# Attention queries kept in both partition halves and split by one operation, and gate tiles dealt by TensorE's work alone

## The chip, the cores and the metric

One core of one Trainium2 chip runs the whole kernel. Time is the device time of one execution in microseconds; a profile of one execution gives the rows below. The engines run side by side and meet at semaphores: TensorE (PE, its weight loads PEld), VectorE (DVE), ScalarE (ACT), GpSimd (POOL) and SyncE (SP), which issues most DMAs.

## The reference, cut to what matters

A decoder layer over 512 tokens of width 2048: a normed input goes through one wide projection; its parts feed sparse attention (16 heads of 64 in 4 groups; compressed, selected and window keys), a spatial-gating MLP and two merge gates; then come cross-attention, a SwiGLU and a last norm. The change touches the attention and the projection of the merge gates that runs beside it.

```python
h = rmsnorm(x, norm_mix_g[l])
proj = h @ w_in[l]
q, kv, nsa_g, u, v, merge_g = jnp.split(proj, split_points, axis=-1)
...
# per query block of 128, per group and head:
s_c = jnp.einsum('bghqd,bgnd->bghqn', qb, kc)
p_c = masked_softmax(s_c, cmp_end[None, :] <= t[:, None])
o_c = jnp.einsum('bghqn,bgnd->bghqd', p_c.astype(vc.dtype), vc)
...
# the same for the selected keys (all blocks here, causal) and the window keys
out = gates[..., 0:1] * unblock(o_c) + gates[..., 1:2] * unblock(o_s) + gates[..., 2:3] * unblock(o_w)
...
g = jax.nn.sigmoid(merge_g).reshape(b, s, N_BRANCHES, D_MODEL)
merged = g[:, :, 0] * (o_a @ w_proj_a[l]) + g[:, :, 1] * (o_b @ w_proj_b[l])
```

## The kernel before

Every float32 operand of a matrix product is split into a high part and a low remainder, and a product is three matmuls: high with high, high with low, low with high. The work is written out by hand, engine by engine; the order on each engine is the order of the code, and semaphores tie the engines together.

Projection phases run one after another: `m0` and the Strassen-like products `g` (which also make the queries and store them to `q_dram`), then `c` (keys and values to be compressed), `k`, `v`, `g` (branch gates), and then the attention stage. A weight panel of 2048 rows by 128 columns is loaded into one of two `raw` slots by SyncE, split in four quarters by VectorE (`split`: a cast at L1504 and a subtraction at L1506) and used by TensorE (L986 to L988). A quarter of the split weights is free again when TensorE has used it.

The attention stage has 128 steps. A unit is two heads of one query block of 128 tokens (`HALVES`, 32 units, 8 for each query block `qi` of 0 to 3); its scores are made in 2, 4, 4 or 5 steps, growing with the causal length (`SCORES`). In each step TensorE does, in this order: a third of the step's gate tiles, the scores of this step (L1194, `scores`), a third of the gate tiles, a turn (`turn_probs`, L1207 and L1210: transposes of scaled probabilities of the unit before), the last third, and `weigh` (L1221 and L1225): the product with the values for what was turned in the step before. Between a turn and its `weigh` ScalarE copies the high part out of the bank (L2474) and VectorE makes the low part (L1763), so `weigh` waits for VectorE.

A gate tile is one k-row of 128 of the merge gates' projection: three matmuls of 512 columns that wait for nothing of the attention. There are 256 of them, 64 quarters, dealt over the 128 steps by `spread` (`TILES_AT`); after each whole quarter VectorE splits the quarter three ahead, at the end of its own work in that step (`QUARTERS_AT`), and after each whole panel ScalarE copies the result (L2311) and stores it. `spread` deals by the mean of two fits: one that evens TensorE's work per step (`step_cost`), one that follows VectorE's work per step (`step_vector`), so that steps in which VectorE has much to do get many tiles and others one or none.

VectorE's order in a step is: row maxima of the scores (L1735), the unit's coefficients (L1747, L1751), the queries' low part for the next unit (`query_low`, L1710), the low part of the turn (L1763), the sum of an output (L1770), splits. ScalarE's is: the queries' high part (`query_high`, L2421, first in a step of `qi` 0, behind the exponentials otherwise), the copy of the turn, the exponentials (L2456), an output copy (L2482), a gate copy. GpSimd scales the probabilities by the coefficients (L2820, L2825).

The keys lie in a tile of 128 partitions, high part in one half and low in the other, so a query has to stand in both halves. Before, `q_t` holds all queries once: partition half `e` is the head `e` of a pair, and one DMA (L785) fills it. For each unit four operations on ScalarE and four on VectorE, each of 64 partitions by 128 columns, take a head from its half and put it into one half of `q_hl`.

Of the kernel before, what the change touches and what calls it, by code (L numbers as in the profile page):

```python
# [162 lines left out]
def step_vector(step):  # L163

    cost = 0
    hu, part = STEP_OF[step] if step < len(STEP_OF) else (len(HALVES), step - len(STEP_OF))
    if step < len(STEP_OF):
        cost += sum(700 + 2 * (NCP if b == CMP else (HALVES[hu][2] + 1) * P) for _, b in SCORES[hu][part])
    if part == 0 and 0 < hu <= len(HALVES):
        cost += 600  # L170
    if hu + 1 < len(HALVES) and part == (0 if len(SCORES[hu]) == 2 else 2):
        cost += 4 * 700
    if step in TURN_AT:
        own, k = TURN_AT[step]
        cost += 460 + 4 * P * max(1, len(turns(HALVES[own][2])[k]))
    if step - 1 in CLOSE_AT:
        cost += 2 * 640
    return cost


def spread(tiles, costs, others):

    each, own = 3 * T, 660

    def even(ratio, other):
        return [max(0.0, (ratio * o - c) / max(each - ratio * w, 1)) for c, o, w in other]

    def fitted(other):
        low, high = 0.0, 2.0 * max(costs) + 4.0 * each
        for _ in range(80):  # L190
            ratio = (low + high) / 2
            low, high = (ratio, high) if sum(even(ratio, other)) < tiles else (low, ratio)
        return even(ratio, other)
    by_pe = fitted([(c, 1, 0) for c in costs])
    by_vector = fitted([(c, o, own) for c, o in zip(costs, others)])
    wanted = [(a + b) / 2 for a, b in zip(by_pe, by_vector)]
    at, left, goal = [], list(range(tiles)), 0.0
    for step, want in enumerate(wanted):
        goal += want
        n = len(left) if step == len(costs) - 1 else min(len(left), max(0, round(goal) - (tiles - len(left))))  # L200
        at.append(left[:n])
        left = left[n:]
    return at
# [33 lines left out]
def build(nc, x, mem, norm_mix_g, w_in, cmp_pe_k, cmp_k_w1, cmp_k_b1, cmp_k_w2, cmp_pe_v, cmp_v_w1,  # L237
# [5 lines left out]
    with ExitStack() as ctx:  # L243
# [53 lines left out]
        q_t = at("q_t", [P, 8, T], F32, C)  # L297
# [328 lines left out]

        def kv_panel(p):
            return (PH["mk"] if p < 4 else PH["mv"],) + PH["mk"].at(p % 4)

        G_UNITS = 7 * G_PAIRS  # L630
        J11, J22, J22S, J12, JZ, J21 = range(1, 7)
        def g_join(what, p):
# [2315 lines left out]
```

## Time and profile before

| what | value |
|---|---|
| median of 3 runs | 2784.32 us (2784.04 to 2785.43) |
| profiled execution, its own time | 2784.62 us |
| its span, first to last instruction | 2782.9 us, 1.7 us less |
| TensorE matmul busy | 2727.8 us, 98% |
| VectorE busy | 2136.2 us, 77% |
| ScalarE busy | 1180.0 us, 42% |
| chain that ended last | TensorE 84%, VectorE 7%, ScalarE 3%, DMA 2%, GpSimd 2% |

The attention stage stands between 481 and 819 us of the span. Busy times of matmuls overlap a little (they are pipelined), so a stall of TensorE is read best from the idle time before its weight loads.

### The profile page before, as it was taken

The page shows a single profiled execution, that of the slowest core. Times are in us where ns is not written, and L with a number is a line of the kernel's source. Part 1 is how long each engine was busy: PE and PEld are TensorE (multiplying, and loading weights), DVE is VectorE, ACT ScalarE, POOL GpSimd, SP SyncE. Part 2 cuts the span into 40 slices and gives each one's busy share as a digit, 9 for nine tenths or more (in the row PEclk, how much of TensorE's full clock was granted, in tenths as well). Part 3 has the DMA queues.
Part 4 walks back from the last instruction along what each step waited for, and adds up shares of the span by engine and source line. Part 5 has one row for each costly group of instructions (what it writes and reads, how often), then busy time and mean ns, then how long its engine had stood idle before and what let it go on. Part 6 is the DMA issues. An engine that isn't in the chain of part 4 may idle for free.

```text
span 2782.9 us, 38124 instructions
## 1 busy us (share of the span) xinstructions
PE 2727.8 (98%) x14157; PEld 2306.9 (83%) x14157; DVE 2136.2 (77%) x3158; ACT 1180.0 (42%) x1935; POOL 449.9 (16%) x414
## 2 busy tenths in 40 slices
PE   8999999999999999999999999999999999999998
PEld 7888887778778888888877888888888888788886
DVE  6777653878764555565678899999999999988887
ACT  6444311656640322211144455555555555443334
POOL 0000020445540454511000000000000000010000
PEclk9999999999999999999999999999999999999999
DMA  7588652222223444544334788888888888899882
GB/s 240 141 188 176 174 144 53 75 73 62 54 68 104 107 130 141 145 120 116 94 118 133 176 204 221 200 217 200 209 217 203 214 202 261 299 293 303 291 267 92
DMA packets 629641, 467.83 MB, mean 168 GB/s; under 512 B 14068, under 2 KB 572008, under 8 KB 623592
## 3 DMA queue, kind: packets, MB, share of 16 engines
q1 hardware_dynamic: 561232, 412.39, 50.2%
q0 software_dynamic: 54736, 34.61, 9.5%
q10 hardware_dynamic: 13512, 18.68, 1.9%
q8 instruction: 102, 1.67, 0.2%
q14 instruction: 59, 0.48, 0.1%
HBM read 404.55 MB, written 61.08 MB: 167 GB/s over the span
## 4 chain that ended last, share of the span: by engine, by line
PE 84%; DVE 7%; ACT 3%; issue 2%; DMA 2%; POOL 2%; ACTq 0%; DVEq 0%; SPq 0%; POOLq 0%
PE banks L986 10%; PE banks L988 10%; PE banks L987 10%; PE banks L1425 9%; PE banks L1422 9%; PE banks L1423 9%; PE banks L1487 4%; PE banks L1488 4%; PE banks L1489 4%; PE banks L1084 2%; PE banks L1087 2%; PE banks L1085 2%; PE banks L1253 1%; PE banks L1254 1%; PE banks L1255 1%
## 5 line engine op out<-in xcount | busy, mean ns | idle before, releaser
L1504 DVE CAST w_hi<-raw 128x512 fp32r<-128x512 f32 (+1 forms) x328 | 186.3, 568 | 304.6 <-PE banks L988 233.1
L986 PE MATMUL banks<-act_hl,w_hi 128*128 128x512 f32 (+1 forms) x944 | 374.5, 397 | 2.4 <-DVE w_lo L1525 2.4
L988 PE MATMUL banks<-act_hl,w_lo 128*128 128x512 f32 (+1 forms) x944 | 368.8, 391 | 0.0
L987 PE MATMUL banks<-act_hl,w_hi 128*128 128x512 f32 (+1 forms) x944 | 368.7, 391 | 0.0
L1423 PEld LDWEIGHTS banks<-t_hl,wf_lo 128*128 128x128 f32 x1312 | 246.5, 188 | 58.3
L1425 PE MATMUL banks<-t_hl,wf_hi 128*128 128x512 f32 x656 | 259.4, 396 | 0.0
L1422 PE MATMUL banks<-t_hl,wf_hi 128*128 128x512 f32 x656 | 259.3, 395 | 0.0
L1506 DVE TENSOR_TENSOR w_lo<-raw,w_hi 128x512 fp32r<-128x512 f32 (+1 forms) x328 | 249.6, 761 | 11.3
L1423 PE MATMUL banks<-t_hl,wf_lo 128*128 128x256 f32 x1312 | 257.7, 278 | 0.0
L1972 DVE TENSOR_TENSOR wf_lo<-raw_f,wf_hi 128x1024 fp32r<-128x1024 f32 x164 | 200.3, 1222 | 56.7 <-ACT wf_hi L2621 56.6
L2621 ACT ACTIVATE wf_hi<-raw_f 128x1024 fp32r<-128x1024 f32 x164 | 173.8, 1060 | 136.9 <-PE banks L1425 83.7
L1423 PEld LDWEIGHTS banks<-tok_hl,wf_lo 128*128 128x128 f32 x984 | 184.8, 188 | 43.7
L1487 PE MATMUL banks<-wo_hi,h_full 128*128 128x512 f32 x560 | 219.0, 391 | 1.4 <-DVE wo_lo L2006 1.4
L1489 PE MATMUL banks<-wo_lo,h_full 128*128 128x512 f32 x560 | 218.0, 389 | 0.0
L1488 PE MATMUL banks<-wo_hi,h_full 128*128 128x512 f32 x560 | 217.9, 389 | 0.0
L988 PEld LDWEIGHTS banks<-act_hl,w_lo 128*128 128x128 f32 (+1 forms) x944 | 176.1, 187 | 39.4
L986 PEld LDWEIGHTS banks<-act_hl,w_hi 128*128 128x128 f32 (+1 forms) x944 | 176.4, 187 | 33.0 <-issue 2.6
L987 PEld LDWEIGHTS banks<-act_hl,w_hi 128*128 128x128 f32 (+1 forms) x944 | 176.6, 187 | 30.3
L1425 PE MATMUL banks<-tok_hl,wf_hi 128*128 128x512 f32 x492 | 194.6, 396 | 0.0
L1422 PE MATMUL banks<-tok_hl,wf_hi 128*128 128x512 f32 x492 | 194.4, 395 | 0.0
L1423 PE MATMUL banks<-tok_hl,wf_lo 128*128 128x256 f32 x984 | 193.3, 278 | 0.0
L2621 ACT ACTIVATE wf_hi<-s 128x1024 fp32r<-128x1024 f32 x123 | 130.2, 1058 | 137.9 <-PE banks L1425 137.9
(361 smaller groups left out, 6142.8 us busy)
## 6 DMA issues: line engine op xcount, KB each, us to landing
raw_f<-in_w_ffn_in_dram SPq DMA_DIRECT2D x82, 1024.0 KB, 9.0
raw<-in_w_in_dram SPq DMA_DIRECT2D x50, 1024.0 KB, 5.6
h_full<-hidden_blocks SPq DMA_DIRECT2D x35, 1024.0 KB, 7.8
wo_raw<-in_w_ffn_out_dram SPq DMA_DIRECT2D x32, 1024.0 KB, 10.0
hidden_blocks<-tok_hl SPq DMA_DIRECT2D x44, 512.0 KB, 6.2
s<-in_w_ffn_in_dram SPq DMA_DIRECT2D x40, 512.0 KB, 5.9
s<-in_w_ffn_in_dram POOLq DMA_DIRECT2D x40, 512.0 KB, 6.5
raw_g<-in_w_in_dram SPq DMA_DIRECT2D x18, 1024.0 KB, 8.8
```

Source lines behind the costliest of these rows:

```text
L986: pe.matmul(dst, w_hi[:, q, j, 0:m], hi, start=first, stop=False)
L987: pe.matmul(dst, w_hi[:, q, j, 0:m], lo, start=False, stop=False)
L988: return pe.matmul(dst, w_lo[:, q, j, 0:m], hi, start=False, stop=last)
L1422: pe.matmul(dst, w_h[:, k], both(k), start=start and k == 0, stop=False, skip_group_check=True)
L1423: mm = pe.matmul(dst[:, 0], w_l[:, k], both(k)[:, 0], start=False, stop=False, skip_group_check=True)
L1425: mm = pe.matmul(dst, w_h[:, k], both(k), start=False, stop=last, skip_group_check=True)
L1487: pe.matmul(dst, hi, wo_hi[g % 3][:, k], start=STARTS[j] and q == 0 and k == 0, stop=False, skip_group_check=True)
L1488: pe.matmul(dst, lo, wo_hi[g % 3][:, k], start=False, stop=False, skip_group_check=True)
L1489: mm = pe.matmul(dst, hi, wo_lo[g % 3][:, k], start=False, stop=last, skip_group_check=True)
L1506: dve.tensor_tensor(w_lo[:, q, :, 0:width], src, w_hi[:, q, :, 0:width].bitcast(F32), ALU.subtract).then_inc(split_done, 1)
L1972: dve.tensor_tensor(wf_lo[g % 3][:].rearrange("p k n -> p (k n)"), src, wf_hi[g % 3][:].rearrange("p k n -> p (k n)").bitcast(F32), ALU.su ...
L2621: act.activation(wf_hi[g % 3][:].rearrange("p k n -> p (k n)"), src, ACT.Copy).then_inc(f_hi, 1)
```

## The change

The queries of a query block are loaded twice, once into each partition half: `q_t` becomes 2 slots (query blocks, in turn) of 16 heads by 128 tokens, the same 16 KiB per partition. Four DMAs on SyncE's queue, each of 64 partitions, fill both slots where one DMA stood; blocks 2 and 3 are loaded by two DMAs each from ScalarE's queue, behind the first high part of blocks 1 and 2. With both heads in both halves, one operation of 128 partitions by 2x128 makes the high part of a unit on ScalarE and one the low part on VectorE. `spread` loses its second fit: tiles are dealt so that TensorE's work by `step_cost` is even over the steps. The number of tiles and of splits is the same.

```diff
@@ step_vector and spread
-def step_vector(step):
-
-    cost = 0
...
-    if hu + 1 < len(HALVES) and part == (0 if len(SCORES[hu]) == 2 else 2):
-        cost += 4 * 700
...
-def spread(tiles, costs, others):
-
-    each, own = 3 * T, 660
...
-    by_pe = fitted([(c, 1, 0) for c in costs])
-    by_vector = fitted([(c, o, own) for c, o in zip(costs, others)])
-    wanted = [(a + b) / 2 for a, b in zip(by_pe, by_vector)]
...
+def spread(tiles, costs):
+
+    each = 3 * T + 96
+    total = sum(costs) + tiles * each
+    at, left, spent = [], list(range(tiles)), 0
+    for step, cost in enumerate(costs):
+        spent += cost
+        goal = total * (step + 1) / len(costs)
+        n = 0 if step < len(costs) - 1 else len(left)
+        while n < len(left) and spent + n * each < goal:
+            n += 1
+        spent += n * each
         at.append(left[:n])
         left = left[n:]
     return at
@@ build: the queries' tile and the dealing
-        q_t = at("q_t", [P, 8, T], F32, C)
+        q_t = at("q_t", [P, 2, HEADS, P], F32, C)
...
-        TILES_AT = spread(GATE_TILES, [step_cost(step) for step in range(STEPS)], [step_vector(step) for step in range(STEPS)])
+        TILES_AT = spread(GATE_TILES, [step_cost(step) for step in range(STEPS)])
...
+        def query(hu):
+            j, pr, qi = HALVES[hu]
+            head = 2 * (2 * j + pr)
+            return q_t[:, qi % 2, head:head + 2]
...
+        q_v = q_dram.rearrange("(a p) t -> p a t", p=HD)
@@ SyncE
-            sp.dma_start(q_t[:], q_dram.rearrange("(k p) t -> p k t", p=P)).then_inc(q_landed, 16)
+            for qi in range(2):
+                for h in range(2):
+                    sp.dma_start(q_t[h * HD:(h + 1) * HD, qi], q_v[:, :, qi * P:(qi + 1) * P]).then_inc(q_landed, 16)
@@ TensorE, scores
-                    pe.wait_ge(q_lo, 4 * hu + 4)
+                    pe.wait_ge(q_lo, hu + 1)
@@ VectorE, query_low
-                for e in range(2):
-                    rows = slice(e * HD, (e + 1) * HD)
-                    for h in range(2):
-                        dve.wait_ge(q_hi, 4 * hu + 2 * e + 2)
-                        dve.scalar_tensor_tensor(out=q_hl[h * HD:(h + 1) * HD, hu % 2, e, 1], in0=q_t[rows, 2 * j + pr, qi * P:(qi + 1) * P],
-                                                 scalar=-HD ** -0.5, in1=q_hl[rows, hu % 2, e, 0].bitcast(F32),
-                                                 op0=ALU.mult, op1=ALU.subtract).then_inc(q_lo, 1)
+                dve.wait_ge(q_hi, hu + 1)
+                dve.scalar_tensor_tensor(out=q_hl[:, hu % 2, :, 1], in0=query(hu), scalar=-HD ** -0.5, in1=q_hl[:, hu % 2, :, 0].bitcast(F32),
+                                         op0=ALU.mult, op1=ALU.subtract).then_inc(q_lo, 1)
@@ ScalarE, query_high
-                if hu == 0:
-                    act.wait_ge(q_landed, G_DMA0 + 16)
+                act.wait_ge(q_landed, G_DMA0 + 32 * max(qi + 1, 2))
                 wait(act, qk_done, STEP0[max(hu - 1, 0)])
-                for e in range(2):
-                    for h in range(2):
-                        act.activation(q_hl[h * HD:(h + 1) * HD, hu % 2, e, 0], q_t[e * HD:(e + 1) * HD, 2 * j + pr, qi * P:(qi + 1) * P], ACT.Copy, scale=-HD ** -0.5).then_inc(q_hi, 1)
+                act.activation(q_hl[:, hu % 2, :, 0], query(hu), ACT.Copy, scale=-HD ** -0.5).then_inc(q_hi, 1)
+                if j == pr == 0 and qi in (1, 2):
+                    act.wait_ge(q_lo, hu)
+                    for h in range(2):
+                        act.dma_start(q_t[h * HD:(h + 1) * HD, (qi + 1) % 2], q_v[:, :, (qi + 1) * P:(qi + 2) * P]).then_inc(q_landed, 16)
```

TensorE, in the steps 93 to 95 of 128 (query block 3). `q_hl` marks the scores, `ident` the turn, `prob_t` the weighing, and three rows with `act_hl` are one gate tile. Before:

```order
3041 L1194 MATMUL banks<-k_win,q_hl 128x512 x2
3042 L1210 MATMUL banks<-ident,prob 128x128 x4
3043 L1225 MATMUL banks<-prob_t,v_hl 128x256 x4
3044 L1194 MATMUL banks<-k_win,q_hl 128x512 x2
3045 L1210 MATMUL banks<-ident,prob 128x128 x4
3046 L1225 MATMUL banks<-prob_t,v_hl 128x256 x4
3047 L986 MATMUL banks<-act_hl,w_hi 128x512
3048 L987 MATMUL banks<-act_hl,w_hi 128x512
3049 L988 MATMUL banks<-act_hl,w_lo 128x512
```

After, the same steps:

```order
2990 L1175 MATMUL banks<-k_win,q_hl 128x512 x2
2991 L967 MATMUL banks<-act_hl,w_hi 128x512
2992 L968 MATMUL banks<-act_hl,w_hi 128x512
2993 L969 MATMUL banks<-act_hl,w_lo 128x512
2994 L1191 MATMUL banks<-ident,prob 128x128 x4
2995 L1206 MATMUL banks<-prob_t,v_hl 128x256 x4
2996 L967 MATMUL banks<-act_hl,w_hi 128x512
2997 L968 MATMUL banks<-act_hl,w_hi 128x512
2998 L969 MATMUL banks<-act_hl,w_lo 128x512
2999 L1175 MATMUL banks<-k_win,q_hl 128x512 x2
3000 L1191 MATMUL banks<-ident,prob 128x128 x4
3001 L1206 MATMUL banks<-prob_t,v_hl 128x256 x4
```

Step 94 had no tile and has one now, and step 93 has one more between its scores and its turn; between the turn of step 93 and the weighing of what it turned, which is the next but one, there is a tile where there was none.

VectorE, in step 92 of the same stage (the step with the queries of the next unit). Before:

```order
988 L1735 ISA banks,attn_max<-banks,causal 128x512
989 L1735 ISA attn_max 128x1
990 L1710 SCALAR_TENSOR_TENSOR q_hl<-q_t,q_hl 64x128 x4
991 L1763 TENSOR_TENSOR prob_t<-banks,prob_t 128x512
992 L1770 TENSOR_TENSOR oa<-banks,o_low 64x128 x2
993 L1504 CAST w_hi<-raw 128x512
994 L1506 TENSOR_TENSOR w_lo<-raw,w_hi 128x512
```

After:

```order
980 L1710 ISA banks,attn_max<-banks,causal 128x512
981 L1710 ISA attn_max 128x1
982 L1686 SCALAR_TENSOR_TENSOR q_hl<-q_t,q_hl 128x2x128
983 L1738 TENSOR_TENSOR prob_t<-banks,prob_t 128x512
984 L1745 TENSOR_TENSOR oa<-banks,o_low 64x128 x2
985 L1485 CAST w_hi<-raw 128x512
986 L1487 TENSOR_TENSOR w_lo<-raw,w_hi 128x512
```

The four query operations have become one in the same place; the rest of this step is as it was.

SyncE, behind the last panel of phase `c`. Before:

```order
56 L783 DMA w_101<-in_cmp_k_w_dram 128x2x64
57 L783 DMA w_101<-in_cmp_v_w_dram 128x2x64
58 L785 DMA q_t<-queries 128x8x512
59 L606 UNCONDITIONAL_BRANCH
60 L606 ISA
```

After:

```order
56 L762 DMA w_101<-in_cmp_k_w_dram 128x2x64
57 L762 DMA w_101<-in_cmp_v_w_dram 128x2x64
58 L766 DMA q_t<-queries 64x16x128 x4
59 L580 UNCONDITIONAL_BRANCH
60 L580 ISA
```

The same 2 MB (two of four query blocks, twice) now come in pieces of 512 bytes instead of 2 KB, ahead of the first panel of phase `k`.

## Rows read from the trace of the kernel before

**Rows 1.** The page, busy time by engine.

```profile
PE 2727.8 (98%) x14157; PEld 2306.9 (83%) x14157; DVE 2136.2 (77%) x3158; ACT 1180.0 (42%) x1935; POOL 449.9 (16%) x414
```

**Rows 2.** Busy times in the attention stage: PE, PEld, DVE, ACT, POOL, clock, DMA.

```profile
480.00:820.00 340.00, 321.70 (x1827) 267.27 (x1825) 268.17 (x878) 208.33 (x672) 167.08 (x193) 1.00 0.22 62
```

**Rows 3.** Waits of the weight loads in the attention stage: us, times, longest.

```profile
PEld banks L1225 <- DVE prob_t L1763: 26.1, 39, 1.4
PEld banks L1207 <- POOL prob_c L2820: 2.6, 6, 0.9
PEld banks L1210 <- POOL prob L2825: 2.1, 4, 0.8
```

**Rows 4.** Timeline of weight loads, steps 93 to 95: start, us, instruction [idle before].

```profile
736.93 0.58 PEld L1210 LDWEIGHTS banks<-ident,prob 128*128 128x128 f32 x4
...
738.30 0.59 PEld L1210 LDWEIGHTS banks<-ident,prob 128*128 128x128 f32 x4
740.25 0.53 PEld L1225 LDWEIGHTS banks<-prob_t,v_hl 128*128 128x128 f32 x4 [1.36 <-DVE prob_t L1763]
...
742.80 0.54 PEld L1225 LDWEIGHTS banks<-prob_t,v_hl 128*128 128x128 f32 x4 [0.49 <-DVE prob_t L1763]
```

**Rows 5.** Timeline of VectorE, end of step 92 and step 93.

```profile
737.21 0.59 DVE L1770 TENSOR_TENSOR oa<-banks,o_low 64x128 f32<-64x128 f32 x2
737.83 0.43 DVE L1504 CAST w_hi<-raw 128x512 fp32r<-128x512 f32 x1
738.29 0.69 DVE L1506 TENSOR_TENSOR w_lo<-raw,w_hi 128x512 fp32r<-128x512 f32 x1
738.90 0.69 DVE L1735 CUSTOM_DVE_ANT_0 banks<-banks,causal 128x512 f32<-128x512 f32 x1
...
739.51 0.69 DVE L1763 TENSOR_TENSOR prob_t<-banks,prob_t 128x512 fp32r<-128x512 f32 x1
```

**Rows 6.** Groups by shape in the stage, 480 to 815 us.

```profile
L1763 DVE TENSOR_TENSOR prob_t<-banks,prob_t 128x512 fp32r<-128x512 f32 x79 | 54.4, 689 | 20.3 <-ACT prob_t L2474 18.8
L2474 ACT ACTIVATE prob_t<-banks 128x512 fp32r<-128x512 f32 x79 | 47.1, 597 | 39.0 <-PE banks L1210 34.1 <-ACT gate_out L2311 2.4 <-PE banks L1225 1.9
L1710 DVE SCALAR_TENSOR_TENSOR q_hl<-q_t,q_hl 64x128 fp32r<-64x128 f32 x124 | 40.8, 329 | 6.9 <-ACT q_hl L2421 3.9
L2421 ACT ACTIVATE q_hl<-q_t 64x128 fp32r<-64x128 f32 x124 | 37.9, 306 | 2.7 <-ACT gate_out L2311 0.4
```

**Rows 7.** The queries' low parts: ns min/median/max, then a quick and a slow unit.

```profile
L1710 DVE SCALAR_TENSOR_TENSOR q_hl<-q_t,q_hl x128: 275/288/815, 457.9 to 786.5; 64x128 fp32r<-64x128 f32 x128
...
482.71 1.24 DVE L1710 SCALAR_TENSOR_TENSOR q_hl<-q_t,q_hl 64x128 fp32r<-64x128 f32 x4
...
773.14 1.76 DVE L1710 SCALAR_TENSOR_TENSOR q_hl<-q_t,q_hl 64x128 fp32r<-64x128 f32 x4
```

**Rows 8.** SyncE's issues at L785 and L746 (first panel of k), each with its landing.

```profile
344.55 0.71 SPq L785 DMA_DIRECT2D q_t<-queries  x1
DMA to landing us min/median/max: 11.7/11.7/11.7
...
346.02 2.25 SPq L746 DMA_DIRECT2D raw<-in_w_in_dram  x1
DMA to landing us min/median/max: 13.8/13.8/13.8
```

**Rows 9.** Windows while queries, then the panel land; the last two columns are DMA share and GB/s.

```profile
350.00:355.00 5.00, 5.00 (x23) 4.13 (x22) 2.01 (x4) 2.37 (x4) 0.00 (x0) 1.00 1.05 386
355.00:360.00 5.00, 5.00 (x24) 4.13 (x22) 0.15 (x1) 0.00 (x0) 0.00 (x0) 1.00 1.19 296
```

**Rows 10.** Timeline of VectorE and ScalarE where phase k begins.

```profile
359.85 0.43 DVE L1504 CAST w_hi<-raw 128x512 fp32r<-128x512 f32 x1 [6.21 <-DMA raw<-in_w_in_dram]
360.31 0.69 DVE L1506 TENSOR_TENSOR w_lo<-raw,w_hi 128x512 fp32r<-128x512 f32 x1
...
363.46 0.59 ACT L2388 ACTIVATE kv_src<-banks 64x512 f32 x1 [8.47 <-PE banks L988]
```

## What the change does to the time, predicted before it ran

> **What bounds the kernel now.** I read the page first, then the waits, and the rows of single steps last. The page shows TensorE busy for 98% of the span [rows 1], so only what TensorE works, or waits for, can move the time. The change takes no matmul away: the same 256 gate tiles, scores, turns and weighings stand in the new order. What it can win is TensorE's idle time in the attention stage, what it can lose is new idle time there or in the phases before.
>
> The window over the stage has TensorE at full clock, 2.4 GHz (granted 1.00), VectorE busy 268.2 of 340 us, ScalarE 208.3, GpSimd 167.1 [rows 2]. No helper is full, yet TensorE waits. Its matmul rows would show 18.3 us idle (340 - 321.7), but a matmul's recorded end hides part of a stall, so I take the waits of the weight loads: 26.1 us in 39 waits of `weigh` for VectorE's low part, and 2.6 + 2.1 us in 10 waits of the turns for GpSimd's scaling, 30.8 us together [rows 3]. That is 1.1% of the span and the most that the stage can give back. Without it a step takes (340 - 30.8) / 128 = 2.4 us on TensorE.
>
> Steps 93 to 95 show how such a wait comes about. After the turn at 738.30 the weights of `weigh` are loaded at 740.25, 1.36 us late, and one step on again 0.49 us late [rows 4]. VectorE meanwhile makes an output sum, a quarter's split (737.83 to 738.98) and the row maxima, and reaches the awaited low part only at 739.51, ending at 740.20 [rows 5]. Step 94 has no gate tile, so TensorE got to its `weigh` with nothing to pass the time. Placing all waits of the stage in the order of steps gives the rule that I rest on: of the 39 waits for VectorE all but one begin in, or right behind, a step with at most one tile. Counted in TensorE's order, 65 of the 128 steps are such steps before (3, 11, 15 and 31 in query blocks 0 to 3, 5 in the steps behind), because the dealing gave the step with the queries and the sums 3 to 5 tiles and its neighbours one or none. So a step with at most one tile costs 26.1 / 65 = 0.40 us.
>
> **The even dealing.** After, 24 steps have one tile, none has none (2, 2, 6, 14 and 0), and 80 have two. From turn to `weigh` the helpers need 0.60 us for the copy and 0.69 us for the low part [rows 6], 1.3 us, plus what VectorE has queued. TensorE meanwhile passes the weighing before, the scores, the next turn and the tiles. Without a tile that is 1.4 us, from the end of the turn's loads at 737.5 to the arrival at 740.25 - 1.36 = 738.9 [rows 4]. A tile adds 0.65 us (23 to 24 matmuls of 512 columns pass in 5 us [rows 9], and a tile is three), so one tile gives 2.05 and two give 2.7 us. Two tiles leave 1.4 us, which covers a split (0.46 + 0.69 us) [rows 5]; one leaves 0.75 us, which does not. I therefore keep the price of 0.40 us for the 24 steps: 9.6 us. Bounds: nothing, if the lighter queries below free VectorE in time; and 26.1 us, if the waits move to the steps with two tiles.
>
> The waits for GpSimd (4.7 us) also fall in steps that TensorE reaches early, after one-tile steps. By the count they would shrink to 24/65, 1.7 us; but units of block 3, where they are longest, now pass in the same time as before or less, and GpSimd's own work is unchanged. I take 3 us, between 1.7 and 4.7.
>
> **The queries' operations.** Per unit four VectorE operations of 64x128 become one of 128x2x128. Four take 1.24 us in a quick unit and 1.76 in a slow one [rows 7]. No row shows the new shape. It has two inputs in SBUF as the old one has. From below it costs as the old one, 0.29 us; from above, twice it with the worst old duration, 1.6 us, hence no gain. The nearest rows are the old 0.29 us for 128 columns and the low part of a turn, 0.69 us for 512: one operation of 256 columns lies between, near 0.42 us. VectorE then has some 0.8 to 1.3 us less per unit, 31 units in the stage, 25 to 40 us; take 29: 239 of 322 us, 74% instead of 79%. On ScalarE four copies of 0.31 us [rows 6] become one of about 0.4 us, 0.8 us less per unit. Neither engine is the bound, so this adds no term of its own: its value is a shorter queue ahead of the low part in one step of each unit, and it cancels what the 80 steps with two tiles might cost (one of 18 such steps waited before, 1.26 us; at that rate 80 would cost 5.6 us).
>
> An operation's length varies: 275 ns at least, 288 in the median, 815 at most [rows 7], the long ones while GpSimd scales probabilities. One operation instead of four can be held up once instead of four times; the worst seen adds 0.53 us, which a step with two tiles bears.
>
> **The queries' load.** This is the part that can cost. SyncE issues the old load at 344.55, it lands after 11.7 us at 356.25, and behind it the first weight panel of phase `k` lands at 359.82 [rows 8]. VectorE waits 6.2 us for that panel and has its first quarter at 361.0; TensorE has finished phase `c` at 363.4, where ScalarE is released [rows 10]. So the panel has 2.4 us of slack, and TensorE stalls by what the panel is later than that. Panel and queries share the DMA engines, which are full: 386 GB/s while the queries move in 2 KB pieces, 296 GB/s while the panel moves in 512-byte pieces [rows 9]. The new load has the same 2.1 MB in 512-byte pieces: at 296 GB/s it takes 7.1 us instead of 5.4, and the panel comes 1.7 us later: no stall. From above, at half that rate (each DMA fills 64 partitions only, and no row shows such a load) 14.2 us, 8.8 us later, a stall of 6.4 us. From below nothing, since an earlier panel helps no one. I take the row of the same piece size, 0, and keep 6.4 as the end. The three more issues (0.37 to 0.71 us each when the queue is free) lie behind transfers that are still running.
>
> A rule of the Trainium skill speaks against that choice: "SBUF — State Buffer", section on the DMA port swizzle, says that partitions 0 to 63 reach only 8 of the 16 ports, measured there as 196 against 328 GB/s for 1 MiB. By it the load would take some 10.7 us, an estimate, the panel would be 5.3 us late, and TensorE would stall 2.9 us. No load of 64 partitions is in this trace, so the row of 296 GB/s neither supports nor refutes it; as a mechanism of this kernel it is rival 2 below.
>
> The four later DMAs on ScalarE's queue are issued one unit ahead; the two issues of a block cost ScalarE some 0.7 us twice, at 61% busy in the stage [rows 2], and their data have a whole query block less one unit to land. The wait for `q_lo` ahead of them is met by VectorE's operation of an earlier step. Both: nothing.
>
> **The sum.** 30.8 us of waits now; 9.6 + 3 us left, so 18.2 us less; load 0. Against the profiled execution's own 2784.62 us that makes 2766.4; the median of the runs is 0.3 us lower, and the forecast is 2766 us.
>
> **The rivals.** A measurement of this kernel tells a change from none at about 0.2%, 5.6 us, so from 2778.7 to 2789.9 is the same.
> 1. Half the gain: the waits for VectorE move to steps with two tiles that also carry a split. For: every second step now carries a split and no step gets extra tiles for it. Against: 1.4 us of room against 1.15 us of split. 0.2 us in each of 80 steps, less the part that the forecast already has, gives 9 us back: 2775.
> 2. The load of 64 partitions at a time runs slower than any row here. Midway between the ends of 0 and 6.4 us TensorE stalls 3 us ahead of `k`, the rest as forecast: 2769, at most 2773. For: every DMA of the stage's rows fills all partitions, and none shows that half of them will do as well. Against: only that the piece size alone explains the row of 296 GB/s.
> 3. No change: the wait is the length of copy and low part, wherever the tiles stand, and moves with them: 2784. Against: steps with 3 to 5 tiles had no wait.
> 4. Slower: VectorE becomes late for good. Its step with the queries has maxima, query, low part, two sums and a split, some 3.2 us, against 2.4 us of TensorE, and no longer 3 or 4 tiles to cover it. If it does not catch up before the next split, each of the 64 quarter splits holds a `weigh` by some 0.6 us: 38 us against 30.8 removed, 2792. It decides from a mean of 30.8 / 64 = 0.48 us per split. Against: VectorE's 74% mean load, and steps without a split that take it 1.3 us.
>
> **How the numbers follow.** Forecast 0.58, rival 1 0.16, rival 2 0.07, rival 3 0.11, rival 4 0.08. Faster: 0.58 + 0.15 + 0.07 = 0.80; the same: 0.11 and a hundredth of rival 1, 0.12; slower 0.08. The forecast's own range is 2758 (all but 4 us of the waits gone) to 2775. For 8 in 10 it takes in rivals 1 and 2 and the edge of 3: 2756 to 2780.
>
> **What would show it.** Right: weight loads in the stage wait under 15 us, most of it in steps with one tile; the stage is about 18 us shorter; the query operations are 31 of 0.4 to 0.5 us on VectorE; the first panel of `k` lands within 2.4 us of its old time and no TensorE wait stands there. Wrong: waits of `weigh` in steps with two tiles, more than 0.1 us each on average; or GpSimd named as the releaser for more than 5 us; or a wait of TensorE for a split at the start of `k`. VectorE's rows at about 0.7 us per query operation would mean that the shape was mis-sized, but not the time.

## The result, and the profile after

The changed kernel takes 2769.37 us in the median of 5 runs (2768.63 to 2771.49), the kernel before 2784.32: a ratio of 0.9946 with an interval of 0.9931 to 0.996, some 15 us less. The forecast was 2766. The profiled execution took 2769.78 us with a span of 2768.1, 14.8 us less than the one before.

The page's engine row of the kernel after answers to [rows 1]: busy time, share of the span, instructions.

```profile
PE 2723.1 (98%) x14157; PEld 2306.4 (83%) x14157; DVE 2113.2 (76%) x3062; ACT 1150.0 (42%) x1839; POOL 455.6 (16%) x414
```

TensorE has the same 14157 matmuls and is still the bound. VectorE has 96 instructions fewer (3158 to 3062), which are the three query operations saved in each of 32 units, and works 23.0 us less; ScalarE has the same 96 fewer.

The window over the attention stage after, columns as in [rows 2]:

```profile
484.00:806.00 322.00, 316.45 (x1832) 266.62 (x1831) 245.84 (x786) 180.11 (x580) 170.94 (x193) 1.00 0.27 72
```

The waits of the weight loads in it, as in [rows 3]: us, times, longest.

```profile
PEld banks L1191 <- POOL prob L2801: 6.0, 12, 1.6
PEld banks L1206 <- DVE prob_t L1738: 5.3, 10, 1.0
PEld banks L1188 <- POOL prob_c L2796: 2.4, 8, 0.4
```

From the first scores to the first weight load behind the stage it was 339.1 us (481.3 to 820.4) and is 320.2 (485.1 to 805.2): 18.9 less. These are the first starts in the rows of the scores and of the phase behind the stage (ns min/median/max, first and last start), before:

```profile
L1194 PEld LDWEIGHTS banks<-k_sel,q_hl x160: 186/188/192, 481.3 to 796.2; 128*128 128x128 f32 x160
L1253 PEld LDWEIGHTS banks<-w_hi,act_hl x128: 187/188/190, 820.4 to 907.6; 128*128 128x128 f32 x128
```

and after:

```profile
L1175 PEld LDWEIGHTS banks<-k_sel,q_hl x160: 186/188/192, 485.1 to 777.6; 128*128 128x128 f32 x160
L1234 PEld LDWEIGHTS banks<-w_hi,act_hl x128: 186/188/190, 805.2 to 892.4; 128*128 128x128 f32 x128
```

The three kinds of waits went from 30.8 to 13.7 us, which is 17.1 of it. But the stage also begins 3.8 us later, so 15.1 us remain for the whole. Two things differ from the forecast in these rows: GpSimd holds more than VectorE does (8.4 against 5.3 us; before it was 4.7 against 26.1), and something ahead of the stage has lost almost 4 us.

That loss stands where phase `k` begins. Windows of the kernel after, while queries and panel land [rows 9] and behind it:

```profile
350.00:355.00 5.00, 5.00 (x23) 4.13 (x23) 2.02 (x4) 2.37 (x4) 0.00 (x0) 1.00 1.21 207
355.00:360.00 5.00, 5.00 (x23) 4.13 (x22) 0.00 (x0) 0.00 (x1) 0.00 (x0) 1.00 1.21 209
...
366.00:368.00 2.00, 2.00 (x7) 1.58 (x8) 1.97 (x3) 0.00 (x0) 2.00 (x3) 0.67 0.54 132
368.00:370.00 2.00, 2.00 (x6) 1.61 (x5) 1.97 (x3) 0.00 (x0) 2.00 (x3) 0.50 0.00 0
370.00:372.00 2.00, 2.00 (x10) 1.55 (x10) 1.97 (x3) 0.00 (x0) 2.00 (x3) 0.97 0.00 0
```

The timeline there, for ScalarE's first copy behind phase `c`, VectorE, TensorE's weight loads and its first matmul [rows 10]:

```profile
363.47 0.59 ACT L2363 ACTIVATE kv_src<-banks 64x512 f32 x1 [8.47 <-PE banks L969]
...
364.63 0.43 DVE L1485 CAST w_hi<-raw 128x512 fp32r<-128x512 f32 x1 [10.97 <-DMA raw<-in_w_in_dram]
365.09 0.69 DVE L1487 TENSOR_TENSOR w_lo<-raw,w_hi 128x512 fp32r<-128x512 f32 x1
...
365.90 0.19 PEld L967 LDWEIGHTS banks<-act_hl,w_hi 128*128 128x128 f32 x1 [2.98 <-ACT kv_src L2364]
...
365.93 0.47 PE L967 MATMUL banks<-act_hl,w_hi 128*128 128x512 f32 x1 [2.58 <-ACT kv_src L2364]
```

The queries move at 207 to 209 GB/s, where they moved at 386 before and where the row of the same piece size had 296. Phase `c` ends at the same time as before (363.47 against 363.46), but the first panel's cast begins at 364.63 instead of 359.85, 4.8 us later. That is more than the 2.4 us of slack, so TensorE idles 2.6 us. The row names ScalarE as the releaser, but the instruction before the restart is VectorE's low part, which ends at 365.78: a wait for several semaphores is put down to one of them, and the one that decided must be read from the times. Behind the idle stretch the granted clock falls to 0.67 and then 0.50, which is 1.2 instead of 2.4 GHz, and is back at 0.97 from 370 on; at those levels 23 matmuls pass in the 6 us shown where some 28 would at the full clock (23 to 24 in 5 us [rows 9]), an estimate of about 1 us, which is the rest of the 3.8.

SyncE's issues, as in [rows 8], show the same from the queue's side. The line for the four query loads: ns min/median/max, first and last start.

```profile
L766 SPq DMA_DIRECT2D q_t<-queries x4: 732/2070/2960, 344.5 to 350.0; - x4
```

The first issue takes 0.73 us, as the one before did (0.71); those behind it, made while the loads ahead of them are under way, take up to 3.0 us. The panel behind them is issued only at 353.2 (before at 346.0).

The query operations themselves, as in [rows 7]: ns min/median/max.

```profile
L1686 DVE SCALAR_TENSOR_TENSOR q_hl<-q_t,q_hl x32: 415/421/894, 462.4 to 765.9; 128x256 fp32r<-128x256 f32 x32
```

On ScalarE the 32 high parts have a median of 403 ns (before 308 for each of 128). Both sizes were forecast (0.42 and about 0.4 us).

### The profile page after: what moved, and what is told of

Read it like the earlier page. It is cut to its first block, busy times and chain, and to the rows that moved or that the text cites. A ratio compares the mean times of both kernels' runs of the same rounds, so it can differ in the third digit from the quotient of the medians.

```text
span 2768.1 us, 37969 instructions
## 1 busy us (share of the span) xinstructions
PE 2723.1 (98%) x14157; PEld 2306.4 (83%) x14157; DVE 2113.2 (76%) x3062; ACT 1150.0 (42%) x1839; POOL 455.6 (16%) x414
## 4 chain that ended last, share of the span: by engine, by line
PE 86%; DVE 5%; ACT 2%; issue 2%; POOL 2%; DMA 2%; ACTq 0%; DVEq 0%; SPq 0%; POOLq 0%
PE banks L967 10%; PE banks L968 10%; PE banks L969 10%; PE banks L1406 9%; PE banks L1403 9%; PE banks L1404 9%; PE banks L1468 4%; PE banks L1469 4%; PE banks L1470 4%; PE banks L1065 2%; PE banks L1068 2%; PE banks L1066 2%; PE banks L1175 1%; PE banks L1206 1%; PE banks L1234 1%
```

## The experiments

Every timed run stands beside runs of the kernel before on the same chip (2785.6 to 2785.8 us); ratios go by those.

**The two halves of the change by themselves.** `queries_alone` is the kernel after with the old dealing; `dealing_alone` is the kernel before with the new one.

```diff
@@ queries_alone, against the kernel after
-        TILES_AT = spread(GATE_TILES, [step_cost(step) for step in range(STEPS)])
+        TILES_AT = spread(GATE_TILES, [step_cost(step) for step in range(STEPS)], [step_vector(step) for step in range(STEPS)])
@@ dealing_alone, against the kernel before: the same line the other way; each with the spread that belongs to it
```

> The changed kernel with the old dealing of gate tiles (the fit that follows VectorE's work is back), so the queries' part alone. Theory A, that the waits of weigh come from steps with at most one gate tile: the 65 such steps are back, the lighter query operations shorten only part of the queue, 20 to 26 us of waits stay in the attention stage, and the load costs its 3.8 us ahead of phase k: 2778 to 2784 us. Theory B, that the four query operations on VectorE and ScalarE were what made TensorE wait: waits near 14 us as in the changed kernel, 2769 to 2773 us.

> The kernel before with the new dealing alone (four query operations per engine and unit, one query load of 2 KB pieces). Theory A (tiles): most of the 30.8 us of waits go, 12 to 18 us stay, no stall ahead of phase k: 2766 to 2772 us. Theory B (query operations): 25 us or more stay, 2779 to 2784 us.

Measured: `queries_alone` 2778.55 us, ratio 0.9974 (0.9964 to 0.9985); `dealing_alone` 2777.28 us, ratio 0.9969 (0.9957 to 0.9982). Waits of the weight loads in the stage, first `queries_alone`:

```profile
PEld banks L1232 <- DVE prob_t L1764: 16.1, 28, 1.4
PEld banks L1214 <- POOL prob_c L2822: 2.8, 6, 0.9
PEld banks L1217 <- POOL prob L2827: 2.1, 4, 0.8
```

and `dealing_alone`:

```profile
PEld banks L1199 <- DVE prob_t L1737: 15.3, 20, 1.8
PEld banks L1184 <- POOL prob L2799: 5.4, 11, 1.5
...
PEld banks L1181 <- POOL prob_c L2794: 1.1, 4, 0.4
PEld banks L1195 <- DVE pc_t L1735: 0.6, 1, 0.6
```

In one table (us; waits are those for VectorE and GpSimd; a wait of 1.1 us for ScalarE's gate copy stands at the end of the stage and is left out):

| kernel | waits for VectorE | for GpSimd | together | stage |
|---|---|---|---|---|
| before | 26.1 | 4.7 | 30.8 | 339.1 |
| queries alone | 16.1 | 4.9 | 21.0 | 329.0 |
| dealing alone | 15.9 | 6.5 | 22.4 | 331.2 |
| both (after) | 5.3 | 8.4 | 13.7 | 320.2 |

Each half takes about 10 and 8 us off the stage, and the two nearly add up (10.1 + 7.9 = 18.0 against 18.9). The forecast had put the whole gain on the dealing. `queries_alone` came out in the range of its theory A, at its low end in waits (21.0 us); `dealing_alone`, at 22.4 us of waits and 2777.28 us, between its two theories.

Placing the waits in the order of steps shows where the dealing fell short. Behind step 19 it does what was forecast: the waits for the low part fall from 21.8 us to 6.6, where the price of 0.40 us for the 22 one-tile steps there would leave 8.8. In steps 7 to 19, in which TensorE weighs units of query block 0, they grow, from 4.1 us to 8.7, although the steps that wait have two or three tiles: 0.73 us in step 7, 0.32 in step 9, then 1.58, 1.58, 1.71, 0.95 and 1.82 in steps 11, 13, 15, 17 and 19. The lighter queries take most of these away: in the kernel after, steps 7 to 19 hold 3.0 us and the rest of the stage 2.3. `queries_alone` bears the dearer load of the queries as well: its TensorE idles 2.3 us ahead of `k`, so its whole-kernel gain (7 us) is smaller than that of its stage (10.1).

**The order of the loads.** `panel_ahead` is the kernel after with the first panel of `k` issued ahead of the four query loads.

```diff
+            keys_panel(0)
             for qi in range(2):
                 for h in range(2):
                     sp.dma_start(q_t[h * HD:(h + 1) * HD, qi], q_v[:, :, qi * P:(qi + 1) * P]).then_inc(q_landed, 16)
-            columns(PH["k"], w_in_v, C_KV + 2 * 256, step=2 * 256)
+            for n in range(1, PH["k"].n):
+                keys_panel(n)
```

> The changed kernel, with the first weight panel of phase k issued ahead of the four query loads on SyncE's queue. Theory P (the load of 64 partitions at 207 GB/s pushes the panel behind TensorE's need): the panel lands near 353 us, no wait of TensorE and no fall of its clock at the start of k, scores begin at 481.3 instead of 485.1 us, 3.8 us less: 2765.6 us. Rival Q (the queries delay some other panel as well, the second of k): the stall moves 11 us on and the time stays near 2769 us.

Measured: 2765.67 us (2765.58 to 2766.82), ratio 0.9927 (0.9913 to 0.994). The panel lands at 355.1 us (expected near 353), TensorE has no wait at the start of `k`, the stage begins at 480.8 instead of 485.1, and its waits are as in the kernel after (13.4 us, stage 319.9). The load costs what stood ahead of `k` and nothing else. A second run of the same kernel and one of the unchanged one came beside later experiments:

> The changed kernel with the first panel of phase k ahead of the query loads once more, as the base of the two kernels with four operations on the same chip: 13.4 us of waits in the stage, ratio to the kernel before 0.9927 to 0.993, about 2765.5 us.

> The changed kernel once more, on the same chip as the three kernels that have its first panel of phase k issued ahead of the query loads, to have its difference to them without a change of chip. By the two profiles (start of the scores 485.1 against 480.8 us, stage 320.2 against 319.9) the changed kernel is 4 us behind a kernel with the panel ahead: ratio to the kernel before 0.9945, about 2769 to 2770.

`panel_again` took 2766.16 us, ratio 0.9931 (0.9918 to 0.9945); `changed_again` 2768.49 us, a little under what was expected, ratio 0.994 (0.9926 to 0.9953). So the order of the loads is worth 2.3 to 3.7 us between medians, which come from different chips; the intervals of the ratios overlap, and it is the trace that settles it. When phase `c` ends differs from one profiled execution to the next, by up to 3.4 us (ScalarE's first copy behind it starts between 362.77 and 366.17 us), so I measure from there to the first scores: 117.1 to 117.2 us in all nine profiled executions of changed kernels without a wait at that place, `panel_ahead` and `panel_again` among them, 117.8 in the kernel before (its 0.7 us stand elsewhere and are open), 121.6 in the kernel after and 119.3 in `changed_again`. In the latter TensorE's weight loads wait 2.2 us and the clock stays up. Its window there:

```profile
365.00:370.00 5.00, 3.76 (x17) 3.14 (x18) 4.90 (x7) 1.89 (x4) 2.99 (x4) 1.00 0.59 143
```

The loss to the clock is thus not part of every execution, and the late panel costs 2.1 us in one and 4.5 us in the other.

**What makes the load slow: half the partitions, or small pieces?** `half_loads` is the kernel before with its one load cut into two of 64 partitions each, pieces of 2 KB as before. `full_width_load` is the kernel after with its four loads spread over all 128 partitions, pieces of 512 bytes as after.

```diff
@@ half_loads
-            sp.dma_start(q_t[:], q_dram.rearrange("(k p) t -> p k t", p=P)).then_inc(q_landed, 16)
+            for h in range(2):
+                sp.dma_start(q_t[h * HD:(h + 1) * HD], q_dram.rearrange("(k p) t -> p k t", p=P)[h * HD:(h + 1) * HD]).then_inc(q_landed, 16)
@@ full_width_load
-                    sp.dma_start(q_t[h * HD:(h + 1) * HD, qi], q_v[:, :, qi * P:(qi + 1) * P]).then_inc(q_landed, 16)
+                    sp.dma_start(q_t[:, qi, h * 8:(h + 1) * 8], q_w[:, :, qi * P:(qi + 1) * P]).then_inc(q_landed, 16)
```

> The kernel before, whose one query load of 128 partitions becomes two DMAs of 64 partitions each, still in 2 KB pieces. Theory P (a DMA into 64 partitions runs at about 207 GB/s whatever its pieces): the queries take some 10 us instead of 5.4, the first panel of k lands 4 to 5 us later, TensorE waits 2 to 3 us and loses about 1 us to a lower clock behind it: 2787 to 2788.5 us. Rival R (the 512-byte pieces were the cause): the load moves at 380 GB/s, the panel keeps its time, 2784.3 us.

> The changed kernel (panel behind the queries) with four DMAs of 512 KB in 512-byte pieces as before, but each into all 128 partitions, so that the queries in the tile are not those that the attention needs. Theory P (half the partitions cost the rate): the four move at 290 GB/s or more, the first panel of k lands by 362 us, no wait of TensorE at the start of k, scores begin near 481 us. Rival R (many small pieces, or four DMAs, cost it): 207 GB/s as with 64 partitions, the panel at 364 us, a wait of 2 to 3 us.

Measured: `half_loads` 2788.69 us, ratio 1.001 (1.0001 to 1.0019). `full_width_load` 2766.9 us in its one run. Windows of `half_loads`:

```profile
350.00:355.00 5.00, 5.00 (x23) 4.13 (x22) 2.24 (x4) 1.71 (x3) 0.00 (x0) 1.00 1.09 220
355.00:360.00 5.00, 5.00 (x23) 4.13 (x22) 0.00 (x0) 0.66 (x2) 0.00 (x0) 1.00 1.07 216
```

and of `full_width_load`:

```profile
350.00:355.00 5.00, 5.00 (x23) 4.13 (x22) 2.00 (x4) 0.00 (x0) 0.00 (x0) 1.00 1.17 303
355.00:360.00 5.00, 5.00 (x24) 4.14 (x23) 1.12 (x2) 2.37 (x4) 0.00 (x0) 1.00 1.20 292
```

Two-kilobyte pieces into 64 partitions move at 216 to 220 GB/s, 512-byte pieces into all partitions at 292 to 303, 512-byte pieces into 64 partitions at 207 to 209. In `queries_alone`, with the same four loads as the kernel after, these same windows show 218 and 217 GB/s, so between piece sizes no difference is seen at 64 partitions. The width of the load decides; the piece size alone would have given the 296 of [rows 9]. That there are four transfers is not the cause either, as `full_width_load` has four. `half_loads` idles TensorE 2.4 us ahead of `k` with nothing else changed, at full clock, where its theory had a fall of the clock as well; its first scores stand 120.1 us behind the end of phase `c`, 2.3 more than before, and it ends 3.1 us slower than the kernel before beside it. `full_width_load` has no wait there, as expected, but two of its expected times were missed: the first panel's cast begins at 364.04 (landing by 362) and the scores at 483.3 (near 481). This execution was 2.8 us late already when it issued the queries (347.3 against 344.5 us), and its first scores stand 117.1 us behind the end of `c`, like those of the kernels without a wait. Of the Trainium skill, "SBUF — State Buffer" says in its section on the DMA port swizzle that the rate of a DMA depends on how many ports its partitions reach, and that 64 partitions reach half of them; its section "Can I just issue two DMAs to hit both halves?" answers that two transfers, one into each half, serialize. Both agree with `half_loads`, whose two loads go to opposite halves and still move at 216 to 220 GB/s together.

**Which engine's query operations held TensorE.** Both kernels are `panel_ahead` with four operations of 64x128 again on one engine only: VectorE in `vector_four`, ScalarE in `scalar_four`.

```diff
@@ vector_four (scalar_four has the same loops around act.activation)
-                dve.scalar_tensor_tensor(out=q_hl[:, hu % 2, :, 1], in0=query(hu), ...
+                for e in range(2):
+                    for h in range(2):
+                        rows = slice(h * HD, (h + 1) * HD)
+                        a = dve.scalar_tensor_tensor(out=q_hl[rows, hu % 2, e, 1], in0=query(hu)[rows, e], ...
```

> Panel ahead, even dealing, queries in both halves; VectorE makes the low part of a unit with four operations of 64x128 again, ScalarE keeps its one. Theory VQ (the queries' part won by VectorE's shorter queue): nearly all of the 8.7 us that the lighter queries were worth under the even dealing (22.4 against 13.7 us of waits) come back: 20 to 22 us of waits, 2772 to 2774 us. Rival SQ (it won by ScalarE's, which also copies the turns): 14 to 16 us, 2766 to 2768 us.

> Panel ahead, even dealing, queries in both halves; ScalarE makes the high part with four operations of 64x128 again, VectorE keeps its one. Theory VQ: 14 to 16 us of waits, 2766 to 2768 us. Rival SQ: 20 us or more, 2772 us or more. If both four-operation kernels lose, each by its share, the chain high part, low part, scores counts, not one engine's queue.

Measured: `vector_four` 2773.6 us, ratio 0.9959 (0.9945 to 0.9972), waits 19.9 us; `scalar_four` 2772.14 us, ratio 0.9951 (0.9937 to 0.9964), waits 19.0. Against `panel_again` beside them (0.9931, 13.4 us) each costs 5.6 to 6.5 us in waits, and 6 to 7.4 us in the median. Of the growth of the waits for VectorE (7.4 and 6.8 us), 4.1 and 4.6 us stand in steps 0 to 15. Theory VQ, that only VectorE's queue counts, fails with `scalar_four`, and its rival SQ with `vector_four`: four operations hurt on either engine alone, and neither of them is full. The same step, 11 of the stage, shows why. VectorE in `panel_ahead`:

```profile
508.18 0.42 DVE L1692 SCALAR_TENSOR_TENSOR q_hl<-q_t,q_hl 128x256 fp32r<-128x256 f32 x1 [0.32 <-ACT q_hl L2399]
508.80 0.69 DVE L1744 TENSOR_TENSOR prob_t<-banks,prob_t 128x512 fp32r<-128x512 f32 x1 [0.20 <-ACT prob_t L2456]
```

VectorE in `vector_four`, and TensorE's weighing behind it:

```profile
511.24 1.30 DVE L1695 SCALAR_TENSOR_TENSOR q_hl<-q_t,q_hl 64x128 fp32r<-64x128 f32 x4 [0.32 <-ACT q_hl L2403]
512.57 0.69 DVE L1748 TENSOR_TENSOR prob_t<-banks,prob_t 128x512 fp32r<-128x512 f32 x1
...
513.32 0.53 PEld L1212 LDWEIGHTS banks<-prob_t,v_hl 128*128 128x128 f32 x4 [1.34 <-DVE prob_t L1748]
```

ScalarE, VectorE and the weighing in `scalar_four`:

```profile
510.29 1.26 ACT L2402 ACTIVATE q_hl<-q_t 64x128 fp32r<-64x128 f32 x4
511.58 0.60 ACT L2460 ACTIVATE prob_t<-banks 128x512 fp32r<-128x512 f32 x1
...
511.58 0.42 DVE L1692 SCALAR_TENSOR_TENSOR q_hl<-q_t,q_hl 128x256 fp32r<-128x256 f32 x1 [1.18 <-ACT q_hl L2402]
512.21 0.69 DVE L1744 TENSOR_TENSOR prob_t<-banks,prob_t 128x512 fp32r<-128x512 f32 x1 [0.20 <-ACT prob_t L2460]
...
512.95 0.53 PEld L1212 LDWEIGHTS banks<-prob_t,v_hl 128*128 128x128 f32 x4 [1.41 <-DVE prob_t L1744]
```

In query block 0 the high part, the low part, the turn's copy and the turn's low part are one chain over both engines. Four operations on VectorE stand ahead of the low part of the turn; four on ScalarE stand ahead of its copy and make VectorE wait 1.18 us for the queries. From the start of the query operation to the one behind it, it is 0.62 us with one operation and 1.33 with four on VectorE, and 0.43 against 1.29 on ScalarE: 0.7 and 0.9 us more. The query operation itself also starts some 0.5 us later against TensorE's scores than in `panel_ahead`. So `weigh`, which has no wait at this step in `panel_ahead`, waits 1.3 to 1.4 us. VectorE's waits for the queries' high part in the stage grow from 1.7 us (5 times) to 12.6 (17 times) in `scalar_four`:

```profile
DVE q_hl L1692 <- ACT q_hl L2402: 12.6, 17, 1.4
```

**What is a tile worth in a step?** Both are `panel_ahead` with another dealing. `refit` has the old fit with the queries' true cost in it, and 54 steps with at most one tile; `two_each` gives every step two tiles.

```diff
@@ refit, in the old step_vector
-        cost += 4 * 700
+        cost += 900
@@ two_each
+    each = tiles // len(costs)
+    return [list(range(step * each, (step + 1) * each)) for step in range(len(costs))]
```

> Panel ahead of the queries, with the old dealing (mean of TensorE's and VectorE's fit) whose cost of the queries is lowered to that of one operation, 900 in place of 2800. It has 54 steps with at most one tile (the old dealing 65, the new 24). Theory A: 54 steps cost what such steps cost beside light queries, 21.0 / 65 = 0.32 us each, 17 us of waits: 2769.5 us. Rival D (the old dealing failed only by its wrong cost of the queries): 10 to 13 us stay, 2762 to 2766 us.

> Panel ahead of the queries, and two gate tiles in every one of the 128 steps (256 tiles) in place of the even dealing. Theory A (waits come in steps with one tile): the 4.7 us of waits that the 24 one-tile steps of the changed kernel hold go, 9 us stay: 2761 us. Rival C (what counts is that TensorE's time per step stays even, since GpSimd's and VectorE's chains have a length of their own): the steps of query block 1 get shorter by 11 tiles in all and wait anew, 14 us or more stay: 2765.5 to 2770 us.

Measured: `refit` 2769.39 us, ratio 0.9942 (0.9929 to 0.9956), 14.2 us of waits (8.9 for VectorE, 5.3 for GpSimd), stage 323.2. At the price of the prediction, 0.40 us a step, 54 steps would have cost 21.6 us for VectorE alone. All 8.9 us do stand in steps with at most one tile, as do all 16.1 us of `queries_alone`; but a step costs 0.16 us in the one (8.9 / 54) and 0.25 in the other (16.1 / 65). The time came out as theory A had it, the waits between both theories. Its stage is 3.3 us longer than that of `panel_ahead`, of which the waits show only 0.8; where the other 2.5 lie is open. `two_each` fits theory A; it took 2762.75 us, ratio 0.9918 (0.9905 to 0.9932), and is the quickest kernel that leaves nothing out. Its waits in the stage:

```profile
PEld banks L1202 <- DVE prob_t L1734: 3.6, 5, 0.9
PEld banks L1187 <- POOL prob L2797: 3.5, 7, 1.2
...
PEld banks L1184 <- POOL prob_c L2792: 0.7, 3, 0.3
```

7.8 us instead of 13.4, stage 317.0 instead of 319.9; here too 2.7 us of the difference are not in these waits. Evening TensorE's work per step is not the best rule either: it still makes 24 steps with one tile, most of them in block 3, where the scores are long and GpSimd's scaling longest, and these 24 steps hold 4.4 of the 13.4 us. The interval of its ratio overlaps that of `panel_ahead` widely; but its slowest run (2763.67 us) is quicker than the quickest of `panel_ahead` (2765.58), and the stage and the waits point the same way.

**GpSimd.** `gpsimd_half` is `panel_ahead` with only the first half of each probability tile's columns scaled.

```diff
-                            pr_rows = prob[:, hu % 2, part - 1, 0:(qi + 1) * P]
+                            pr_rows = prob[:, hu % 2, part - 1, 0:(qi + 1) * P // 2]
```

> Panel ahead of the queries, and GpSimd scales only the first half of each probability tile's columns (the other half keeps unscaled values). Theory G (what is left of the waits is mostly GpSimd's chain, 8.3 of 13.4 us): the waits of turns for GpSimd go to under 1 us, those of weigh for VectorE stay at 4 to 5 us: 2757 to 2758.5 us. Rival V (TensorE then only arrives sooner at the same VectorE queue): GpSimd's waits turn into waits for VectorE, 2762 to 2765 us.

Measured: 2760.57 us, ratio 0.991 (0.9895 to 0.9925), stage 314.8. Its waits:

```profile
PEld banks L1212 <- DVE prob_t L1744: 3.3, 5, 1.0
PEld banks L1194 <- POOL prob_c L2802: 2.0, 7, 0.4
...
PEld banks L1208 <- DVE pc_t L1742: 0.6, 1, 0.6
...
PEld banks L1197 <- POOL prob L2807: 0.3, 1, 0.3
```

The waits for the scaled probabilities fall from 5.9 to 0.3 us, those for `prob_c`, whose scaling is unchanged, hardly move (2.3 to 2.0), those for VectorE fall from 5.2 to 3.9, and the stage is 5.1 us shorter. The time lies between both theories. So these waits are the length of GpSimd's own work and not only coefficients that come late; and they are the largest single item that the change leaves (6.0 us).

## Why the prediction was right, and where it was not

**What bounds the kernel, and by how much.** Right. TensorE's waits in the stage, read at the weight loads, were nearly the whole of what there was to win. Against the kernel before, the stage of every timed kernel here changed by what these waits lost, within 2 us (before to after: 18.9 against 17.1); between two of the changed ones up to 2.7 us are not in them. The 18.3 us of idle matmul time in [rows 2] would have been too small a purse to pay this gain from and leave 13.7 us over.

**The sum.** 12.6 us of waits were forecast to be left and 13.7 are; the stage was to be 18 us shorter and is 18.9; the total misses by the load, 3 us. The good sum of the waits is in part luck: those for VectorE are 4.3 us fewer than forecast (5.3 for 9.6), those for GpSimd 5.4 us more (8.4 for 3), and what the lighter queries gave made up for what the dealing did not. Three terms were off, and the load besides.

**The even dealing** was to take 16.5 us off the waits for VectorE and 1.7 off those for GpSimd. Alone it takes 10.2 off the first (26.1 to 15.9) and adds 1.8 to the second. The price of 0.40 us for a step with at most one tile, and nothing for one with two, held in kind behind step 19 and failed ahead of it: it counted tiles, while the wait also depends on what VectorE and ScalarE have queued in the step. With the old queries, steps with two tiles that weigh units of block 0 wait up to 1.82 us (`dealing_alone`); with the new ones, the 24 steps with one tile hold only 1.5 of the 5.3 us for VectorE. The sign that the prediction named for itself, waits mostly in one-tile steps, did not show: of the 13.7 us they hold 4.4. Two of the signs named for a wrong forecast did show: GpSimd as the releaser for more than 5 us, and a wait of TensorE at the start of `k`.

**The queries' operations** were the step that failed: "Neither engine is the bound, so this adds no term of its own". The sizes of one operation were right to 10 ns (VectorE's rows in the stage fall from 40.8 to 14.2 us, 26.6 where 29 were taken), and the 96 instructions fewer are worth 10.1 us of the stage by themselves (`queries_alone`), 8.7 us of waits beside the new dealing (22.4 to 13.7). They stand in the chain from a turn to its weighing, on both engines, and shorten it by 0.8 us where it is late (`vector_four`, `scalar_four`). A mean load of 74% says nothing of that. The text had weighed this as a cancellation of what steps with two tiles might cost, 5.6 us at most, taken from one step that waited among 18; only three of those 18 stood in block 0.

**GpSimd** was to leave 3 us, at most 4.7, and leaves 8.4. The argument that shorter units of block 3 would press on it was made and then given too little. Its work is unchanged and TensorE now comes sooner.

**The load** was taken as nothing, between 0 and 6.4 us. It costs about 3 us (2.3 to 3.7 between medians; 2.1 and 4.5 in the two profiled executions, the latter with the fall of the clock). Rival 2 was right in mechanism and size: its 3 us, and a panel 4.8 us late against the 5.3 worked out beside it. The row of 296 GB/s, full-width pieces of the same size, was the wrong neighbour. The estimate from the Trainium skill ("SBUF — State Buffer", the section on the DMA port swizzle), a stall of 2.9 us, agrees with the 2.6 us measured. The slack of 2.4 us, read from [rows 8, 10], was right. The issues on ScalarE's queue took 0.68 us each, two for a block as forecast; their data landed within 8.2 us and nobody waited.

**The rivals.** Rival 1 (waits move to two-tile steps with a split) holds in kind but not in size: 3.8 us of the waits for VectorE stand in steps with two or three tiles, each in or behind a step with a split, not 16. Rival 3 is refuted by the 17.1 us, rival 4 by the 10 waits that are left. Four of these 10, 3.0 of the 5.3 us, stand in steps 13 to 19, the other six behind. The timeline of VectorE, ScalarE and the weighing at step 17 of the kernel after:

```profile
526.35 0.69 DVE L1487 TENSOR_TENSOR w_lo<-raw,w_hi 128x512 fp32r<-128x512 f32 x1
526.96 0.19 DVE L1710 CUSTOM_DVE_ANT_0 banks<-banks,cmp_mask 128x32 f32<-128x32 f32 x1
...
529.25 0.60 ACT L2286 ACTIVATE gate_out<-banks 128x512 f32<-128x512 f32 x1
529.88 0.35 ACTq L2288 DMA_DIRECT2D merge_gates<-gate_out  x1
530.33 0.60 ACT L2450 ACTIVATE prob_t<-banks 128x512 fp32r<-128x512 f32 x1 [0.48 <-ACT gate_out L2286]
...
530.96 0.69 DVE L1738 TENSOR_TENSOR prob_t<-banks,prob_t 128x512 fp32r<-128x512 f32 x1 [1.71 <-ACT prob_t L2450]
...
531.70 0.53 PEld L1206 LDWEIGHTS banks<-prob_t,v_hl 128*128 128x128 f32 x4 [0.96 <-DVE prob_t L1738]
```

A split (to 526.96) delays the next row maxima, these the exponentials, and ScalarE then has a gate copy to make and to store (529.25 to 530.23) before it copies the turn at 530.33. VectorE, named as the releaser, had itself stood idle for 1.71 us: the wait at `weigh` is then ScalarE's in this step, though the row says VectorE.

## What to carry to other kernels

An engine's mean load does not price an edit. Ask whether the operation stands between a producer and the one that the bound engine awaits, and count the whole chain over all engines in it; there 0.8 us for each of 31 units, on an engine that is 61% busy, was worth about 6 us over a stage. A rule drawn from one order of the work (waits per tile count) holds only with the queues that it was counted in; when a change edits both, run each alone. And before a load is cut differently, compare its width in partitions as well as its pieces, and send the transfer that is awaited first ahead of it.

## What the runs showed of the hardware that was not expected

A load into 64 partitions moved at 207 to 220 GB/s with either piece size (`half_loads`, `queries_alone` and the kernel after), one into 128 at 292 to 303 with the same 512-byte pieces and 386 with 2 KB [rows 9]. SyncE's issues of it took 0.73 to 2.96 us where the one issue before took 0.71 [rows 8], and held back the issue of the panel by 7 us. One VectorE operation of 128x256 took 421 ns in the median against 288 for 64x128 with half the columns, the same on ScalarE 403 against 308, so that one for four saves some 0.8 us on each. The granted clock fell to 0.50 behind a weight-load gap of 3.0 us in the kernel after, and stayed at 1.00 behind gaps of 2.2, 2.3 and 2.4 us at the same place in `changed_again`, `queries_alone` and `half_loads`.
